# Score blocks sharing one tile in the mixers of a two-layer diffusion trunk, with a reordered output projection

## The chip, the cores and the metric

The kernel runs on 1 core of one Trainium2 chip, as one launch. The metric is the device time of that launch in microseconds, lower is better. Every matmul works in fp32 or in the split form described below.

## The reference

One inference step of a trunk with two layers over 640 tokens (512 latent tokens of the sample, 128 context tokens of the prompt), width 1024. Layer 0 mixes tokens with HGRN2 (8 heads, 128 wide), layer 1 with GLA (4 heads, keys 128 wide, values 256 wide). Each mixer is a gated linear recurrence, run forward and backward, and followed by a gated norm over each head and an output projection; then comes PEER, a product-key layer of single-neuron experts. Cut to what matters here:

```
S_t = diag(exp(g_t)) S_{t-1} + k_t v_t^T ;  o_t = S_t^T q_t      (both directions, summed)
y   = o * rsqrt(mean(o*o over the head) + EPS) * w * silu(gate)  (_gated_head_norm)
x   = x + g1 * (y @ w_out)                                       (output projection)
q   = h @ w_q; top 16 of keys per half and head; 16 of the 256 sums; gates = softmax
x   = x + g2 * sum_e gates_e * gelu(u_e . h) * v_e               (PEER)
```

Outputs are the two normed token blocks and the final states of the context scans.

## The kernel before, in words

Tokens stand in five tiles of 128 (`NT` = 5, the last is the context), the width in eight chunks of 128 (`DC` = 8). The stages run one after the other, each in a block of its own, with a barrier between: setup, then for each layer a mixer, `mix_out`, retrieve, route and experts, and finish at the end. A product that needs fp32 precision at a faster rate is split: both factors are cut into a high part and a low rest, both float32r, and three matmuls (high by high, high by low, low by high) add up in PSUM.

**Mixer.** A loop runs over the heads (`pe.Fori`, L1163), each engine in its own written order. For a head, TensorE projects this head and part of the next, transposes, updates the states, and then does the attention. Inside a tile of 128 tokens the decayed scores are not one product. For each of seven levels (64, 32, 16, 8, 4, 2, 1) there is a pair of factors in `ex`, exact for token pairs whose indices differ first in that bit; `scores(t)` (L1132) makes seven full 128x128 products (L1137) and one for the diagonal (L1138), side by side in `pA[t % 2]`. VectorE multiplies all eight tiles at once by 0/1 masks in `level_mask` (L1048), into `am`. TensorE then takes the eight masked tiles, for each of `NV` value chunks (1 in HGRN2, 2 in GLA), as eight accumulating matmuls against the turned values, and two more against the states (L1154). The order is scores(0), scores(1), outputs(0), scores(2), outputs(1) and so on. ScalarE copies each output tile away (L856). After its last mask VectorE goes on with the decays of the next head (L966, then scans).

**`mix_out`.** ScalarE and VectorE square alternate chunks of the mixer output into two buffers `sq`; TensorE sums them by one-column matmuls into `rows` (L1291), all 8 (or 4) heads; VectorE inverts, ScalarE roots. `spread(g)` (L1301) turns the root of head g into a full tile by 5 fp32 matmuls. VectorE multiplies by it and by the norm weight (L1350), then by the gate (L1364), ScalarE takes the high part (L1272), VectorE the low (L1358). The gate is made by ScalarE's sigmoid (L1255, two buffers `sg`) and GpSimd (L1233). The product with `w_out` (L1308) runs in two ways: for the first `AHEAD` = 3 of eight column groups TensorE follows the chunks k as they come (18 matmuls of 320 columns per k); the other five follow group by group (48 matmuls each), with weights split by ScalarE (L1248) and GpSimd (L1228) into three buffers.

**Experts.** At the start TensorE turns the context tokens of h row-wise: 32 transposes of `h_hi` and `h_lo` (L2069), whose halves VectorE copies and adds (L1982, L1984) in turn; then the first u block is transposed (L2127), and the main loop runs over 128 blocks of experts. At its end ScalarE (L1964) and VectorE (L2049) copy the six halves of `py`, TensorE transposes them (L2142), VectorE adds to x (L2054), ScalarE squares it (L1969) and GpSimd sums the squares in `acc` (L1926), with a drain behind each of its seven additions.

Of the kernel before, what the change touches and what calls it, by code (L numbers as in the profile page):

```python
# [15 lines left out]
P = 128  # L16
# [11 lines left out]
NL = len(LEVELS)  # L28
DEPTH = 2
# [5 lines left out]
TG = 2  # L35
# [63 lines left out]
def build_program(nc, a, out, upto=99):  # L99
# [6 lines left out]
    with ctx:  # L106
        c = {}
        for name, shape, dt in [
            ("ident", [P, P], F32), ("ones_d", [P, P], F32), ("ones_h", [P, P], F32),
            ("level_mask", [P, (NL + 1), P], BF16), ("scan_f", [P, T], BF16), ("scan_b", [P, T], BF16),  # L110
            ("vec", [P, 3 * P], F32), ("mod", [P, DEPTH, 48, 2], F32), ("one", [P, 1], F32),
            ("scale_w", [P, DC, 2], F32), ("lb", [P, 16], F32), ("oml", [P, 16], F32),
# [49 lines left out]
def setup(nc, a, c, x_sp, x_saved):  # L162
# [4 lines left out]
    with ExitStack() as s:  # L167
# [81 lines left out]
        def _(act):  # L249
# [3 lines left out]

            for g in range(3 + 10):
# [8 lines left out]
        def _(dve):  # L263
# [6 lines left out]
            for l, m in enumerate(LEVELS):  # L270
                nc.vector.tensor_scalar(low[:, :], xorf[:, :], float(m), None, ALU.is_ge)
                dve.drain()
                nc.vector.scalar_tensor_tensor(c["level_mask"][:, l, :], xorf[:, :], float(2 * m), low[:, :],
                                               ALU.is_lt, ALU.mult)
                dve.drain()
            nc.vector.tensor_scalar(c["level_mask"][:, NL, :], xorf[:, :], 0.0, None, ALU.is_equal)
# [220 lines left out]
def mixer(nc, a, c, mx, h_hi, h_lo, og_sp, out, layer, x_saved):  # L497
# [19 lines left out]
    with ExitStack() as s:  # L517
# [17 lines left out]
        am = [sb(f"am{i}", [P, NL + 1, P]) for i in range(2)]  # L535
# [352 lines left out]
        def _(dve):  # L888
# [81 lines left out]
            def head(h, final):  # L970
# [73 lines left out]
                for t in range(NT):  # L1044
# [3 lines left out]
                    nc.vector.tensor_mul(am[t % 2][:, :, :], pA[t % 2][:, :, :], c["level_mask"][:, :, :]) \  # L1048
# [21 lines left out]
        def _(pe):  # L1070
# [24 lines left out]
            def head(h, final):  # L1095
# [36 lines left out]
                def scores(t):  # L1132
# [3 lines left out]
                    for l in range(NL):  # L1136
                        nc.tensor.matmul(pA[t % 2][:, l, :], ex[:, 1, l, tok], ex[:, 0, l, tok], start=True, stop=True)  # L1137
                    nc.tensor.matmul(pA[t % 2][:, NL, :], kd[:, tok], q[:, tok], start=True, stop=True) \  # L1138
# [3 lines left out]
                for t in range(NT):  # L1142
# [5 lines left out]
                    for vv in range(NV):  # L1148
                        dst = pO[:, vv, :]
                        terms = [(tt[:, 10 + t * NV + vv, :], am[t % 2][:, l, :]) for l in range(NL + 1)]  # L1150
# [18 lines left out]
def mix_out(nc, a, c, mx, h_hi, h_lo, og_sp, x_sp, layer):  # L1169

    NV, H = mx.nv, mx.heads
    AHEAD = 3
    w_out = a["gla_w_out" if mx.gla else "hgrn_w_out"][0].rearrange("(k p) n -> p k n", p=P)
    gw = VEC["gla_g" if mx.gla else "hgrn_g"]
    oT, inv = c["x"], c["inv"][:, 0:H * NT]
    with ExitStack() as s:
# [5 lines left out]
        sg = [sb(f"sg{i}", [P, T]) for i in range(2)]  # L1182
        sq = [sb(f"sq{i}", [P, T]) for i in range(2)]
# [4 lines left out]
        spread_s = ps("spread_s", [P, 4, P])  # L1188
        spread_c = ps("spread_c", [P, P])
        pp = [[ps(f"pp{j}_{i}", [P, 512]) for i in range(2)] for j in range(AHEAD)]  # L1190
        (sq_act, sq_dve, summed, inverted, rooted, spread_done, spread_read, sig_done, gate_done, y_done, hi_done,
         lo_done, w_hi_done, w_lo_done, proj, added, x_ready, squared) = (sem(n) for n in (
            "sq_act", "sq_dve", "summed", "inverted", "rooted", "spread_done", "spread_read", "sig_done", "gate_done",
# [5 lines left out]
        rows = pp[0][0][:, 0:H * NT]  # L1199

        @block.sync
        def _(sp):
# [20 lines left out]
        def _(pool):  # L1223
# [11 lines left out]
            for k in range(DC):  # L1235
                gate(k)
                if k < AHEAD:
                    low(k)
# [998 lines left out]
```

## Time and profile before

| | |
|---|---|
| median of 3 runs | 4647.11 us (4644.31 to 4648.92) |
| the profiled execution, its own time | 4647.06 us |
| its span in the trace | 4645.2 us |
| mixer, layer 0 and layer 1 | 568.4 and 460.9 us |
| `mix_out`, layer 0 and layer 1 | 124.0 and 115.9 us |
| experts, layer 0 and layer 1 | 1221.7 and 1220.2 us |
| setup, retrieve, route and finish together | 934.1 us |

The stages stand in a row, so their times add up to the span. The engine columns of the page are busy time over the whole span; inside a stage the bound changes from place to place, and timelines of the stage show it. A timeline row gives the start in us, the duration, the engine, the line, the operation with output and inputs, the shapes and, in brackets, the idle time before it with the instruction that ended it. PE is TensorE, PEld its weight load, DVE VectorE, ACT ScalarE, POOL GpSimd.

### The profile page before, as it was taken

Reading aid. Unit: us, or ns where it says so; the run is one execution under the profiler, and the core shown is the slowest. Engines: PE = TensorE matmul, PEld = TensorE weight load, DVE = VectorE, ACT = ScalarE, POOL = GpSimd, SP = SyncE. Lnnn points to the kernel's source line nnn. Section 1 sums busy time; section 2 is a strip of 40 time slices with the busy share of each in tenths; the row PEclk is TensorE's granted clock in tenths of the full one; section 3 lists DMA queues with packets and bytes.
Section 4 is the critical chain, followed back from the end, with each engine's and each line's share of the span. In section 5 each row is a group of like instructions: output and inputs, shape, how many; then the busy total and the mean of one; then the engine's idle time right before and its main releaser. Section 6 shows DMA issues by size and latency. Waiting matters only on the chain. (4 is left out here: it accounts for less than half of the span.)

```text
span 4645.2 us, 72467 instructions
## 1 busy us (share of the span) xinstructions
PE 4146.5 (89%) x24511; PEld 3755.6 (81%) x24511; DVE 3803.5 (82%) x6733; ACT 1642.9 (35%) x2307; POOL 1991.1 (43%) x1435
## 2 busy tenths in 40 slices
PE   7799986877799999999996888786889999999997
PEld 3599986875699999999986778785779999999996
DVE  7688884599788888999996876378978888899997
ACT  7545442213233333333334432221323333333333
POOL 3234331215454545566544221220744545565663
PEclk9899998888899999999997988897999999999998
DMA  9411112214999999999972110220699999999995
GB/s 368 146 46 55 54 33 74 60 31 91 270 366 360 364 360 358 366 362 362 363 281 81 38 40 20 82 66 16 148 316 363 362 362 363 356 365 363 361 361 207
DMA packets 616027, 1049.49 MB, mean 226 GB/s; under 512 B 229699, under 2 KB 388870, under 8 KB 615430
## 3 DMA queue, kind: packets, MB, share of 16 engines
q1 hardware_dynamic: 467814, 508.86, 32.4%
q0 software_dynamic: 147456, 536.94, 31.1%
q10 hardware_dynamic: 672, 2.62, 0.2%
q8 instruction: 46, 0.75, 0.1%
q14 instruction: 39, 0.32, 0.0%
HBM read 982.75 MB, written 65.54 MB: 226 GB/s over the span
## 5 line engine op out<-in xcount | busy, mean ns | idle before, releaser
L1920 POOL DMA_INDIRECT rows_ex<-in_peer_v,ctx_index x512 | 707.6, 1382 | 475.5 <-DVE row_acc_ex L1999 359.9
L1920 POOL DMA_INDIRECT rows_ex<-in_peer_u,ctx_index x512 | 588.0, 1148 | 645.4 <-DVE dots_ex L2002 501.7
L2088 PE MATMUL pu_ex<-h_hi,uT_hi_ex 128*128 128x384 f32 x2048 | 715.6, 349 | 1.9 <-ACT coef_ex L1944 1.0
L1999 DVE SCALAR_TENSOR_TENSOR row_acc_ex<-rows_ex,factor_ex,row_acc_ex 128x1024 f32<-128x1024 f32 x512 | 657.6, 1284 | 52.8 <-issue 11.1
L2088 PE MATMUL pu_ex<-h_hi,uT_lo_ex 128*128 128x384 f32 x2048 | 692.6, 338 | 0.0
L2088 PE MATMUL pu_ex<-h_lo,uT_hi_ex 128*128 128x384 f32 x2048 | 692.5, 338 | 0.0
L2096 PE MATMUL py_ex<-v_hi_ex,c_hi_ex 128*128 128x512 f32 x1536 | 622.4, 405 | 0.0
L2002 DVE CUSTOM_DVE_ANT_0 rows_ex<-rows_ex,h_row_ex 128x1024 f32<-128x1024 f32 x512 | 604.3, 1217 | 0.0
L2096 PE MATMUL py_ex<-v_lo_ex,c_hi_ex 128*128 128x512 f32 x1536 | 601.0, 391 | 0.0
L2096 PE MATMUL py_ex<-v_hi_ex,c_lo_ex 128*128 128x512 f32 x1536 | 600.6, 391 | 0.0
L1933 ACT ACTIVATE uT_hi_ex<-pT_ex 128x512 fp32r<-128x512 f32 x512 | 304.1, 594 | 575.1 <-PE pT_ex L2081 473.0
L1990 DVE TENSOR_TENSOR uT_lo_ex<-pT_ex,uT_hi_ex 128x512 fp32r<-128x512 f32 x512 | 351.7, 687 | 166.4 <-ACT uT_hi_ex L1933 153.7
L1939 ACT ACTIVATE v_hi_ex<-v_raw_ex 128x1024 fp32r<-128x1024 f32 x256 | 271.7, 1061 | 485.8 <-PE py_ex L2096 485.8
L2088 PEld LDWEIGHTS pu_ex<-h_hi,uT_hi_ex 128*128 128x128 f32 x2048 | 385.9, 188 | 12.8 <-DVE uT_lo_ex L1990 1.5
L2088 PEld LDWEIGHTS pu_ex<-h_lo,uT_hi_ex 128*128 128x128 f32 x2048 | 386.3, 189 | 9.8
L2088 PEld LDWEIGHTS pu_ex<-h_hi,uT_lo_ex 128*128 128x128 f32 x2048 | 385.4, 188 | 0.0
L2096 PEld LDWEIGHTS py_ex<-v_lo_ex,c_hi_ex 128*128 128x128 f32 x1536 | 288.3, 188 | 63.8
L2096 PEld LDWEIGHTS py_ex<-v_hi_ex,c_lo_ex 128*128 128x128 f32 x1536 | 289.5, 188 | 42.9
L2096 PEld LDWEIGHTS py_ex<-v_hi_ex,c_hi_ex 128*128 128x128 f32 x1536 | 288.8, 188 | 42.4
L2013 DVE TENSOR_TENSOR v_lo_ex<-v_raw_ex,v_hi_ex 128x1024 fp32r<-128x1024 f32 x256 | 311.7, 1218 | 0.0
L2081 PE MATMUL pT_ex<-ident,u_raw_ex 128*128 128x128 f32 x2040 | 306.1, 272 | 3.1 <-issue 3.1
L2081 PEld LDWEIGHTS pT_ex<-ident,u_raw_ex 128*128 128x128 f32 x2040 | 253.7, 140 | 46.5 <-issue 3.7
(418 smaller groups left out, 8599.6 us busy)
## 6 DMA issues: line engine op xcount, KB each, us to landing
u_raw_ex<-in_peer_u SPq DMA_DIRECT2D x256, 512.0 KB
v_raw_ex<-in_peer_v SPq DMA_DIRECT2D x256, 512.0 KB
ada<-in_ada_w SPq DMA_DIRECT2D x24, 2048.0 KB, 10.0
gates<-stage_ro SPq DMA_DIRECT2D x12, 4096.0 KB, 23.3
g_raw_ex<-gates SPq DMA_DIRECT2D x256, 192.0 KB
w_raw_hgrn<-in_hgrn_w_in SPq DMA_DIRECT2D x40, 512.0 KB
w_raw_re<-in_peer_w_q SPq DMA_DIRECT2D x32, 512.0 KB, 3.7
w_raw_gla<-in_gla_w_in SPq DMA_DIRECT2D x25, 512.0 KB
```

Source lines behind the costliest of these rows:

```text
L1920: pool.indirect_dma_start(out=rows[m % RING][:, :], out_offset=None, in_=a["peer_u" if m < TG * NC else "peer_v"].rearrange("l n d -> (l n ...
L1933: act.activation(uT_hi[b][:, 4 * part:4 * part + 4, :], pT[:, :, :], ACT.Copy) \
L1939: act.activation(v_hi[b][:, :], v_raw[b][:, :], ACT.Copy).then_inc(v_hi_done, 1)
L1990: nc.vector.tensor_sub(uT_lo[b][:, at, :], pT[:, :, :], uT_hi[b][:, at, :].bitcast(F32)) \
L1999: nc.vector.scalar_tensor_tensor(row_acc[g][:, :], rows[j][:, :], factor[:, j:j + 1], row_acc[g][:, :], ALU.mult, ALU.add).then_inc(row_fr ...
L2002: nc.vector.tensor_tensor_reduce(rows[j][:, :], rows[j][:, :], h_row[g][:, :], 1.0, 0.0, ALU.mult, ALU.add, accum_out=dots[:, j:j + 1]).th ...
L2013: nc.vector.tensor_sub(v_lo[b][:, :], v_raw[b][:, :], v_hi[b][:, :].bitcast(F32)).then_inc(v_lo_done, 1)
L2081: last_ = nc.tensor.transpose(pT[:, k, :], u_raw[b][:, (4 * part + k) * P:(4 * part + k + 1) * P], c["ident"][:, :])
L2088: last_ = nc.tensor.matmul(pu[:, 0:TD], w[:, k, :], x[:, k, 0:TD], start=(k == 0 and w is uT_hi[b] and x is h_hi), stop=(k == DC - 1 and w ...
L2096: last_ = nc.tensor.matmul(py[2 * t + i][:, :], w[:, t * P:(t + 1) * P], x[:, i * HALF_D:(i + 1) * HALF_D], start=(first and w is c_hi[b] ...
```

## The change

Four places are edited.

1. **Mixer.** `scores(t)` puts levels 64, 32 and 16 into one tile, as eight smaller matmuls that write only the blocks which these levels own: two 64x64 blocks off the diagonal for level 64, two 64x64 blocks on it for level 32, and four 32x32 blocks on the diagonal over them for level 16. `level_mask`, `am` and the output terms have six tiles instead of eight.
2. **`mix_out`.** `AHEAD` is 2; each `sq` and `sg` has a buffer per chunk, so squares and sigmoids wait for no reader; the sums are made and rooted in two halves; `spread` has two buffers and runs two heads ahead; gate and norm weight are applied ahead on DVE (`gated`).
3. **Experts, start.** The 32 transposes become 32 float32r matmuls against `ident_r`, with high and low part added in PSUM, in four banks of their own; ScalarE copies them.
4. **Experts, end.** The copies of `y` are split three and three, the transposes begin after three of them and have four targets, GpSimd's additions carry their semaphore themselves, without the drain.

In route, the two `stage` buffers are allocated first, which moves addresses only.

```diff
-            ("level_mask", [P, (NL + 1), P], BF16), ("scan_f", [P, T], BF16), ("scan_b", [P, T], BF16),
+            ("level_mask", [P, NM, P], BF16), ("scan_f", [P, T], BF16), ("scan_b", [P, T], BF16),
...
+            nc.vector.tensor_scalar(c["level_mask"][:, 0, :], xorf[:, :], 16.0, None, ALU.is_ge)
...
-                    for l in range(NL):
-                        nc.tensor.matmul(pA[t % 2][:, l, :], ex[:, 1, l, tok], ex[:, 0, l, tok], start=True, stop=True)
+                    blocks = [(0, 64 * b, 64 - 64 * b, 64) for b in range(2)] + [(1, 64 * b, 64 * b, 64) for b in range(2)]
+                    blocks += [(2, 32 * b, 32 * b, 32) for b in range(4)]
+                    for l, r, col, n in blocks:
+                        nc.tensor.matmul(pA[t % 2][r:r + n, 0, col:col + n], ex[:, 1, l, t * P + r:t * P + r + n],
+                                         ex[:, 0, l, t * P + col:t * P + col + n], start=True, stop=True)
+                    for l in range(3, NL):
+                        nc.tensor.matmul(pA[t % 2][:, l - 2, :], ex[:, 1, l, tok], ex[:, 0, l, tok], start=True, stop=True)
...
-    AHEAD = 3
+    AHEAD = 2
+    GROUP = H // 2
...
             gates(0)
+            gates(1)
             weights(0)
             weights(1)
-            gates(1)
-            weights(2)
             gates(2)
...
+            for g in range(GROUP):
+                sums(g)
             spread(0)
+            spread(1)
+            for g in range(GROUP, H):
+                sums(g)
             for k in range(DC):
-                if k % NV == NV - 1 and k // NV + 1 < H:
-                    spread(k // NV + 1)
-                if k == 0:
-                    pe.wait_ge(w_lo_done, AHEAD)
                 pe.wait_ge(lo_done, k + 1)
                 for j in range(AHEAD):
+                    if k == 0:
+                        pe.wait_ge(rooted, j + 1)
+                        pe.wait_ge(w_lo_done, j + 1)
...
+                if k % NV == NV - 1 and k // NV + 2 < H:
+                    spread(k // NV + 2)
...
+            def gated(k):
+                dve.wait_ge(gate_done, k + 1)
+                nc.vector.scalar_tensor_tensor(oT[:, k, :], oT[:, k, :], c["vec"][:, gw + k % NV:gw + k % NV + 1],
+                                               og[:, k, :], ALU.mult, ALU.mult)
...
             for k in range(DC):
                 normal(k)
-                dve.wait_ge(gate_done, k + 1)
-                dve.drain()
-                nc.vector.tensor_mul(y[k % 3][:, :], y[k % 3][:, :], og[:, k, :]).then_inc(y_done, 1)
+                if k == 0:
+                    inverse(1)
+                if k + 3 < DC:
+                    gated(k + 3)
                 if k >= 1:
                     low(k - 1)
+                dve.drain()
...
-                pool.tensor_tensor(c["acc"][:, :], c["acc"][:, :], rows[k % 2][:, 0:T], ALU.add)
-                pool.drain().then_inc(gathered, 1)
+                if k >= 2:
+                    pool.wait_ge(gathered, k - 1)
+                pool.tensor_tensor(c["acc"][:, :], c["acc"][:, :], rows[k % 2][:, 0:T], ALU.add).then_inc(gathered, 1)
...
-                for w, part in enumerate((h_hi, h_lo)):
-                    for k in range(4):
-                        last_ = nc.tensor.transpose(py[2 * (n % 2) + w][:, k * P:(k + 1) * P],
-                                                    part[:, 4 * half + k, tok].bitcast(F32), c["ident"][:, :])
+                for k in range(4):
+                    for w, part in enumerate((h_hi, h_lo)):
+                        last_ = nc.tensor.matmul(py[n][:, k * P:(k + 1) * P], part[:, 4 * half + k, tok],
+                                                 c["ident_r"][:, :], start=(w == 0), stop=(w == 1))
```

The order of ScalarE in `mix_out` is now: the squares, sigmoids 0 to 3, the high parts of weight groups 0 and 1, sigmoids 4 to 7, the first root, the high part of chunk 0, the second root, then the other high parts.

TensorE, first attention of HGRN2, before and of the change (`pA` holds the scores, `pO` the outputs):

```order
L1137 MATMUL pA_hgrn<-ex_hgrn 128x128 x7
L1138 MATMUL pA_hgrn<-q_hgrn,kdiag_hgrn 128x128
L1137 MATMUL pA_hgrn<-ex_hgrn 128x128 x7
L1138 MATMUL pA_hgrn<-q_hgrn,kdiag_hgrn 128x128
L1145 REGISTER_ALU
L1154 MATMUL pO_hgrn<-am_hgrn,tt_hgrn 128x128 x8
L1154 MATMUL pO_hgrn<-e_hgrn,S_hgrn 128x128 x2
```

```order
L1145 MATMUL pA_hgrn<-ex_hgrn 64x64 x4
L1145 MATMUL pA_hgrn<-ex_hgrn 32x32 x4
L1148 MATMUL pA_hgrn<-ex_hgrn 128x128 x4
L1149 MATMUL pA_hgrn<-q_hgrn,kdiag_hgrn 128x128
L1145 MATMUL pA_hgrn<-ex_hgrn 64x64 x4
L1145 MATMUL pA_hgrn<-ex_hgrn 32x32 x4
L1148 MATMUL pA_hgrn<-ex_hgrn 128x128 x4
L1149 MATMUL pA_hgrn<-q_hgrn,kdiag_hgrn 128x128
L1156 REGISTER_ALU
L1165 MATMUL pO_hgrn<-am_hgrn,tt_hgrn 128x128 x6
L1165 MATMUL pO_hgrn<-e_hgrn,S_hgrn 128x128 x2
```

Three full products of a score call have become eight small ones, and two output terms are gone.

TensorE in the first `mix_out`, from the sums to the first products, before and of the change:

```order
L1291 MATMUL pp_0_mo<-ones_d,sq_mo 128x1 x40
L1301 MATMUL spread_s_mo<-ident,inv 128x128 x4
L1301 MATMUL spread_c_mo<-ident,inv 128x128
L1301 MATMUL spread_s_mo<-ident,inv 128x128 x4
L1301 MATMUL spread_c_mo<-ident,inv 128x128
L1308 MATMUL pp_0_mo<-h_hi,w_hi_mo 128x320
L1308 MATMUL pp_0_mo<-h_lo,w_hi_mo 128x320
```

```order
L1297 MATMUL pp_0_mo<-ones_d,sq_mo 128x1 x20
L1306 MATMUL spread_s_mo<-ident,inv 128x128 x4
L1306 MATMUL spread_c_mo<-ident,inv 128x128
L1306 MATMUL spread_s_mo<-ident,inv 128x128 x4
L1306 MATMUL spread_c_mo<-ident,inv 128x128
L1297 MATMUL pp_0_mo<-ones_d,sq_mo 128x1 x20
L1313 MATMUL pp_0_mo<-h_hi,w_hi_mo 128x320
L1313 MATMUL pp_0_mo<-h_lo,w_hi_mo 128x320
```

The second half of the sums now stands behind the first two spreads.

## Rows read from the trace of the kernel before

**Rows 1.** The page: busy time, share of the span and instructions of each engine

```profile
PE 4146.5 (89%) x24511; PEld 3755.6 (81%) x24511; DVE 3803.5 (82%) x6733; ACT 1642.9 (35%) x2307; POOL 1991.1 (43%) x1435
```

**Rows 2.** Timeline of PE, hgrn attention of one head (start us, us, instruction, idle before)

```profile
392.41 1.80 PE L1137 MATMUL pA_hgrn<-ex_hgrn 128*128 128x128 f32 x14 [0.86 <-DVEq L1043]
...
394.27 1.73 PE L1137 MATMUL pA_hgrn<-ex_hgrn 128*128 128x128 f32 x14
...
396.05 1.95 PE L1154 MATMUL pO_hgrn<-am_hgrn,tt_hgrn 128*128 128x128 f32 x16
```

**Rows 3.** Timeline of DVE there: the mask multiply

```profile
408.31 1.23 DVE L1048 TENSOR_TENSOR am_hgrn<-pA_hgrn,level_mask 128x1024 f32<-128x1024 f32 x1 [2.01 <-PE pA_hgrn L1138]
```

**Rows 4.** Timeline of PE, gla attention: two score calls in turn

```profile
2592.65 1.73 PE L1137 MATMUL pA_gla<-ex_gla 128*128 128x128 f32 x14
...
2598.90 1.73 PE L1137 MATMUL pA_gla<-ex_gla 128*128 128x128 f32 x14
```

**Rows 5.** Timeline of PE in setup, where small and full tiles alternate

```profile
142.15 1.05 PE L378 MATMUL pc<-fold,mod_row 4*128 4x2 f32 x8
143.13 1.09 PE L389 MATMUL pa<-ada_hi,cs 128*4 128x512 f32 x4
```

**Rows 6.** Groups of weight loads in setup, by form (busy us, mean ns)

```profile
L378 PEld LDWEIGHTS pc<-fold,mod_row 4*128 4x128 f32 x8 | 1.0, 186 | 0.5 <-issue 0.5
L389 PEld LDWEIGHTS pa<-ada_lo,cs 128*4 128x4 f32 x8 | 0.6, 84 | 1.4 <-DVE ada_lo L313 0.6
```

**Rows 7.** Engines' busy time in mix_out's first stretch; last PEclk, DMA share, GB/s

```profile
730.60:749.70 19.10, 17.19 (x90) 16.81 (x90) 3.91 (x7) 7.04 (x9) 0.48 (x1) 0.59 0.96 357
```

**Rows 8.** Timeline of PE in mix_out

```profile
731.39 14.68 PE L1291 MATMUL pp_mo<-ones_d,sq_mo 128*128 128x1 f32 x80 [2.03 <-ACT sq_mo L1260]
...
762.48 0.63 PE L1308 MATMUL pp_mo<-h_hi,w_hi_mo 128*128 128x320 f32 x1 [9.22 <-POOL w_lo_mo L1228]
...
767.44 1.49 PE L1301 MATMUL spread_s_mo<-ident,inv 128*128 128x128 f32 x8
...
780.14 0.42 PE L1308 MATMUL pp_mo<-h_hi,w_hi_mo 128*128 128x320 f32 x1 [2.75 <-DVE h_lo L1358]
...
782.88 1.05 PE L1301 MATMUL spread_s_mo<-ident,inv 128*128 128x128 f32 x8
...
786.91 0.42 PE L1308 MATMUL pp_mo<-h_hi,w_hi_mo 128*128 128x320 f32 x1 [2.75 <-DVE h_lo L1358]
...
814.66 0.41 PE L1308 MATMUL pp_mo<-h_hi,w_hi_mo 128*128 128x320 f32 x1 [1.91 <-POOL w_lo_mo L1228]
```

**Rows 9.** Timeline of DVE in mix_out, one step of the k loop

```profile
790.97 0.75 DVE L1350 SCALAR_TENSOR_TENSOR y_mo<-x,vec,spread_s_mo 128x512 f32<-128x512 f32 x1 [4.11 <-PE spread_c_mo L1301]
791.63 0.34 DVE L1350 SCALAR_TENSOR_TENSOR y_mo<-x,vec,spread_c_mo 128x128 f32<-128x128 f32 x1
792.06 0.82 DVE L1364 TENSOR_TENSOR y_mo<-y_mo,og_mo 128x640 f32<-128x640 f32 x1
792.81 0.82 DVE L1358 TENSOR_TENSOR h_lo<-y_mo,h_hi 128x640 fp32r<-128x640 f32 x1
```

**Rows 10.** Timeline of PE in mix_out, second layer

```profile
2952.06 0.64 PE L1308 MATMUL pp_mo<-h_hi,w_hi_mo 128*128 128x320 f32 x1 [12.82 <-POOL w_lo_mo L1228]
```

**Rows 11.** Timeline of PE at the start of experts

```profile
1230.56 1.09 PE L2069 MATMUL py_ex<-ident,h_hi 128*128 128x128 f32 x4 [9.66 <-PEq L57]
...
1239.02 0.81 PE L2127 MATMUL pT_ex<-ident,u_raw_ex 128*128 128x128 f32 x4 [2.04 <-issue]
```

**Rows 12.** Timeline of ACT after the last product of experts

```profile
2426.27 2.06 ACT L1964 ACTIVATE u_raw_ex<-py_ex 128x512 f32<-128x512 f32 x4 [6.45 <-PE py_ex L2096]
```

**Rows 13.** Timeline of POOL at the end of experts

```profile
2432.22 1.54 POOL L1926 TENSOR_TENSOR acc<-acc,rows_ex 128x640 f32<-128x640 f32 x1 [22.16 <-ACT rows_ex L1969]
2441.16 1.54 POOL L1926 TENSOR_TENSOR acc<-acc,rows_ex 128x640 f32<-128x640 f32 x1 [7.40 <-issue]
2442.87 1.53 POOL L1926 TENSOR_TENSOR acc<-acc,rows_ex 128x640 f32<-128x640 f32 x1 [0.18 <-issue]
```

More of the change, by code:

```diff
@@ L28 @@
 NL = len(LEVELS)
+NM = NL - 1
 DEPTH = 2
@@ L534, in mixer @@
         ex = sb("ex", [P, 2, NL, T])
-        am = [sb(f"am{i}", [P, NL + 1, P]) for i in range(2)]
+        am = [sb(f"am{i}", [P, NM, P]) for i in range(2)]
         tt = sb("tt", [P, NTR, P])
@@ L1149, in head @@
                         dst = pO[:, vv, :]
-                        terms = [(tt[:, 10 + t * NV + vv, :], am[t % 2][:, l, :]) for l in range(NL + 1)]
+                        terms = [(tt[:, 10 + t * NV + vv, :], am[t % 2][:, l, :]) for l in range(NM)]
                         if t < NT - 1:
@@ L1181, in mix_out @@
         og = sb("og", [P, DC, T])
-        sg = [sb(f"sg{i}", [P, T]) for i in range(2)]
-        sq = [sb(f"sq{i}", [P, T]) for i in range(2)]
+        sg = sb("sg", [P, DC, T])
+        sq = sb("sq", [P, DC, T])
         y = [sb(f"y{i}", [P, T]) for i in range(3)]
@@ L1198, in mix_out @@
         block = s.enter_context(nc.Block())
-        rows = pp[0][0][:, 0:H * NT]
+        rows = [pp[j][0][:, 0:GROUP * NT] for j in range(2)]
+        inv = [c["inv"][:, j * GROUP * NT:(j + 1) * GROUP * NT] for j in range(2)]
         @block.sync
@@ L1229, in low @@
                                    w_hi[j % AHEAD][:, :, :].bitcast(F32), ALU.subtract).then_inc(w_lo_done, 1)
-            def gate(k):
+            for k in range(DC):
                 pool.wait_ge(sig_done, k + 1)
-                pool.tensor_tensor(og[:, k, :], og[:, k, :], sg[k % 2][:, :], ALU.mult).then_inc(gate_done, 1)
[L1235 to L1238, printed above, removed]
+                pool.tensor_tensor(og[:, k, :], og[:, k, :], sg[:, k, :], ALU.mult).then_inc(gate_done, 1)
+                if k in (1, 2):
+                    low(k - 1)
             for j in range(AHEAD, DC):
@@ L1285, in _, with sums @@
         def _(pe):
-            for g in range(H):
+            def sums(g):
                 for k in range(g * NV, (g + 1) * NV):
@@ L1579, in route @@
         ALLC = [P, NT, PH, TOPK]
+        stage = [sb(f"stage{i}", [P, KEYS, STORE]) for i in range(2)]
         e = sb("e", ALLC)
@@ L1598, in route @@
             [shared[:, i * UNIT * P:(i + 1) * UNIT * P].rearrange("p (u n) -> p u n", n=P) for i in range(2)]
-        stage = [sb(f"stage{i}", [P, KEYS, STORE]) for i in range(2)]
         pg = [ps(f"pg{i}", [P, UNIT, P]) for i in range(2)]
```

155 lines of the change are left out of this document (78 added, 77 removed).

## The prediction

> **What bounds the kernel now.** I read the page first, then stage by stage the timelines of the engines. TensorE is busy 89% of the span [rows 1], but that is a mean over stages: in the expert loops it never stops and the change leaves them alone. The edits touch four places, and what counts there is who is waited for.
>
> In the HGRN2 attention TensorE runs without a gap from score call to score call: a call starts at 394.27 and its outputs at 396.05, so a call takes 1.79 us for 16 fp32 passes (a full fp32 matmul is two passes in the trace), 0.112 us each; before the phase it has idled 0.86 us for VectorE [rows 2]. The phase leads somewhere: the last mask, 1.23 us on VectorE [rows 3], releases the decays of the next head, a chain that ends in those 0.86 us. So this head's time from first score to last mask is on the path, TensorE's work behind it is not. In GLA one token tile takes 6.25 us (2592.65 to 2598.90, [rows 4]), all TensorE, and the next projection waits for the end of the phase, so there all of it is on the path.
>
> `mix_out` is bound by latencies. It begins with DMA at 0.96 of its share and a granted clock of 0.59, a mix of 2.4 GHz and 1.2 GHz [rows 7]. TensorE makes its sums from 731.39 for 14.68 us, has spread the first head by 749.70 (the stretch of [rows 7] ends there), later waits 9.22 us for the low weights from GpSimd and starts its first product at 762.48. In the k loop it is idle 2.75 us of a step of 6.77 us (780.14 to 786.91) for `h_lo`, since spread, norm, gate, high and low follow each other [rows 8].
>
> **The change, part by part.** The sum is made against the profiled execution, 4647.06 us by its own time, span 4645.2; the median shown is 4647.11, so the two can be taken as one. 0.2%, about what a measurement of this kernel can tell from no change, is 9.3 us.
>
> *Score calls.* Removed: three full matmuls, 6 passes, 0.67 us. Added: eight matmuls on 64 columns and on 32, 16 passes. The trace shows no such matmul. If a pass shrinks with its columns, 8 x 0.056 + 8 x 0.028 = 0.67 us: nothing won or lost. To this comes the change of tile shape: in setup, eight passes of another shape take 0.98 us from start (142.15) to the next row (143.13) where 8 x 0.112 would be 0.89, so about 0.09 us for a change of shape [rows 5]. A call has three such changes (full to 64, 64 to 32, 32 to full): 0.27 us. The weight load is no reason for more: it takes 84 ns for 4 columns and 186 ns for 128 [rows 6], so it shrinks with the columns too. I take +0.4 us per call, c below: 0.27, and something for calls that run at 1.2 GHz and for passes that shrink less than their columns. Bounds: if blocks for different output partitions run side by side, 8 + 8 passes cost as 4 + 2 or so, about 0.30, and c is 0.30 + 0.27 - 0.67 = -0.1; if no pass falls below a full one, c is 10 x 0.112 + 0.27 = +1.39.
>
> The Trainium skill ("TensorEngine Tiling (Array Packing)", Key Properties) says that changing the tiling mode drains TensorE; this trace agrees, with about 0.09 us a change. The Trainium skill ("TensorE: Matmul & The Clock Gate", Part 3: Packing small matmuls) says that matmuls on different column tiles overlap; that is rival B, and where the sum has -7 us for the mixers, -37 would stand. No row here shows two blocks at once.
>
> *Mask and outputs.* The mask works on 768 instead of 1024 columns: 1.23 us becomes about 0.93, 0.30 less. Outputs lose two matmuls per value chunk, 4 passes, 0.45 us. In HGRN2 between first score and last mask lie five score calls, three output groups and the last mask: 5c - 3 x 0.45 - 0.30 = 5c - 1.64 per head, 8 heads. In GLA, TensorE alone counts: 5c - 5 x 2 x 0.45 = 5c - 4.48, 4 heads. Together 60c - 31 us; **with c = 0.4, -7 us**. The masks in setup cost nothing: VectorE waits there for inputs.
>
> *`mix_out`, first layer.* The start gets no shorter. ScalarE now does all eight sigmoids and two weight copies before its root, but that ends no later than the sums and the loads let it: I put the first root at 747.4: the sums end at 746.07 now (731.39 + 14.68), and the root follows a microsecond later. At 1.2 GHz two spreads follow, 2.6 us each, and 40 passes of sums at 0.213, 8.5 us: 761.1. Then inverse, root, norm and low of VectorE (one step costs 0.75 + 0.34 + 0.82 + 0.82 us [rows 9]) give the first product at 765.4, 3 us later than before. Step 0 of the loop takes 3.2 + 2.6 us, step 1 3.2 + 1.4 (12 matmuls, and a spread), the next four 1.76 + 1.37 each (12 x 0.147, which is what 6.77 - 2.75 - 1.37 leaves for each of 18, and a spread of 1.37 us with its start-up [rows 8]), the last two 1.76: 26.4 us. Gone are the idle 2.75 us per step, since two heads are spread ahead and gates are applied ahead; late next is VectorE at 2.7 us a step, which stays under 3.1. Loop end 791.8. Then a wait for weights, 1.91 us before at 814.66 [rows 8], with two buffers about 2.9, then six groups instead of five, 48 x 0.147 = 7.04 us each, 42.3; three us for the last sums of x: 840, where the stage ended at 854.6. **-14.6 us**. The trade is a group of column work moved from the loop (it filled idle time there) to the end, +7, against a loop of 26 instead of 50 us.
>
> *`mix_out`, second layer.* Here a head has two chunks. The first product stands at 2952.06 [rows 10], 37.8 us into the stage, and comes at the same 34.8 us as above, 2949.1. The loop is then bound by VectorE, eight steps of 2.7 and the ends: 23 us. With 2.9 + 42.3 + 3 the stage ends at 3019.8 instead of 3030.1, **-10.3 us**.
>
> *Start of experts.* TensorE needs from 1230.56 for groups of four transposes about 0.86 us each, with stops for VectorE's adds, and starts on u at 1239.02 after 2.04 us of idle time [rows 11]. A float32r matmul is one quick pass: in `mix_out` 18 of them with 320 columns fill 762.48 to 767.44 at 1.2 GHz [rows 8], 0.27 us each, so 128 columns take about 0.11, where a transpose takes 0.21 ((1.09 - 0.45) / 3 in the group of four). With the loads I take 0.13 us for each of 32, and nothing waits between: done at about 1234.9, and u has landed. **-4.1 us per layer, -8.2**; the copies on ScalarE lie beside the transposes of u. The expert loop behind is TensorE's alone, so the shift comes through.
>
> *End of experts.* ScalarE copies four halves in 2.06 us [rows 12]; TensorE now starts after two, 1.0 us earlier. GpSimd's first addition starts at 2432.22 and the second at 2441.16, 7.40 us after it has ended, though ScalarE's squares come every 1.1 us; the later ones are 1.71 apart, with 0.18 between [rows 13]. What stands between the first two is the drain. Without drains the adds follow at about 1.6, but the block ends with one, and I suppose that GpSimd pays there what it paid at the first: something that the gathers left to be cleared. Then 1.0 + 6 x 0.11 is all: **-1.7 us per layer, -3.4**. If it vanishes, 7.2 us more per layer.
>
> **Sum:** -7 - 14.6 - 10.3 - 8.2 - 3.4 = -43.5, from 4647.06: **4603.5 us**.
>
> **The rivals.**
>
> *The drain's price goes away* (A). For it: the wait sits right behind the first drain and nowhere else, as if the drain itself were at fault. Against: it would be long even if only the gathers' remains were waited for, and somebody must wait for them. It gives 2 x 7.2 less, 4589.
>
> *Blocks run side by side* (B). For it: they write different partitions; against: no row shows it, and the two 64-column blocks of level 64 and those of level 32 alternate over the same partitions. c = -0.1, mixers -37 instead of -7: 4573.
>
> *The loop of `mix_out` gains nothing* (C). For it: TensorE's second sums stand before the first product, ScalarE's sigmoids before the first root; if the gates' loads come late, both slip, and GpSimd's gates slow VectorE in the loop. Against: DMA is done by 749 and GpSimd's gates now begin 10 us earlier. Without the 25: 4628.
>
> *Slower: small passes cost full ones* (D). Each of the 16 passes takes 0.112 us plus three changes of shape, c = 1.39 and 60c - 31 = +52: 4663. It decides from c = 1.28 on, where the mixers' loss passes the 36.5 us won elsewhere by 9.3. For it: in setup eight passes of two columns take 0.98 us, no less than full ones would. Against: those have weights of 128 columns and 0.112 is then the load; here the weights have 64 or 32, and loads of 4 columns take less than half.
>
> *It does not do what it says* can hardly be: the written orders show the blocks and the six terms. A scheduler stands nowhere between.
>
> **How the numbers follow.** My sum 0.55, A 0.18, B 0.09, C 0.10, D 0.06, no effect 0.02. The range takes in A, B and C, and the unknown c up to about 0.9: 4570 to 4632. Faster by over 0.2% needs c under 0.97 with the rest as summed, or c under 0.55 without `mix_out`: 0.89; within 0.2% 0.05; slower 0.06.
>
> **What would show it.** Right: a score call of about 2.2 us in HGRN2, blocks' rows of some 0.03 to 0.06 us apart, the period 4.0 (+0.4 - 0.45); first product of `mix_out` 35 us into the stage and steps of 3.1 us; in experts u transposed from 1235 less what came before; on GpSimd seven additions without a hole, and a long drain at the end of the block. Wrong: score calls over 3 us, or under 1.8; a first product of `mix_out` later than 40 us; retrieve, route or the expert loop of another length than before.

## The result, and the profile after

The changed kernel takes 4583.27 us (median of 4 runs, 4577.81 to 4585.24) against 4647.7 us; the ratio is 0.9861, 95% interval [0.9844, 0.9878]. That is 64 us less, where 43.5 were forecast. The profiled execution took 4584.52 us by its own time, span 4582.7.

```profile
span 4582.7 us, 73015 instructions
PE 4118.9 (90%) x24791; PEld 3713.0 (81%) x24791; DVE 3765.7 (82%) x6718; ACT 1645.2 (36%) x2314; POOL 1991.2 (43%) x1435
```

These are the page's lines that answer to [rows 1]. They say little: 280 more PE records, 28 us less busy. The stages say it all. Each is taken from its first to its last record in both traces:

| stage | before | after | difference | forecast |
|---|---|---|---|---|
| mixer, layer 0 | 568.4 | 560.4 | -8.0 | +2.9 |
| `mix_out`, layer 0 | 124.0 | 120.9 | -3.1 | -14.6 |
| route, layer 0 | 171.3 | 161.8 | -9.5 | 0 |
| experts, layer 0 | 1221.7 | 1220.7 | -1.0 | -5.8 |
| mixer, layer 1 | 460.9 | 446.7 | -14.2 | -9.9 |
| `mix_out`, layer 1 | 115.9 | 103.7 | -12.2 | -10.3 |
| route, layer 1 | 172.0 | 161.6 | -10.4 | 0 |
| experts, layer 1 | 1220.2 | 1218.9 | -1.3 | -5.8 |
| setup, retrieve, finish, and the steps between stages | 590.8 | 588.0 | -2.8 | 0 |

(The forecast of the mixers is its formula at c = 0.4: 8 x 0.36 and 4 x -2.48.) The total came out near because an edit that I had costed at nothing, the place of route's buffers, gave 20 us, while `mix_out` in layer 0 and the experts gave little of what they were to give. A stage in a single trace is good to some 3 us: in six traces whose mixers are the same code (the change and experiments 1, 2, 6, 7 and 8) the first takes 557.3 to 560.4 us and the second 443.7 to 447.0.

**The score call.** TensorE in one HGRN2 attention, the answer to [rows 2]:

```profile
392.23 0.65 PE L1145 MATMUL pA_hgrn<-ex_hgrn 128*64 128x64 f32 x16
392.81 1.16 PE L1148 MATMUL pA_hgrn<-ex_hgrn 128*128 128x128 f32 x8
393.81 0.39 PE L1149 MATMUL pA_hgrn<-q_hgrn,kdiag_hgrn 128*128 128x128 f32 x2
394.03 1.50 PE L1165 MATMUL pO_hgrn<-am_hgrn,tt_hgrn 128*128 128x128 f32 x12
395.37 0.61 PE L1165 MATMUL pO_hgrn<-e_hgrn,S_hgrn 128*128 128x128 f32 x4
395.91 0.28 PE L1145 MATMUL pA_hgrn<-ex_hgrn 128*64 128x64 f32 x2
```

From the first of the 16 block passes to the first full pass behind them it is 0.58 us (392.23 to 392.81), 0.036 us each: less than the 0.67 us that passes one after another would need, even with no price for a change of shape. The single records of this call show why. The 64-column passes start in pairs 0.007 us apart (four pairs, 0.05 to 0.10 us between), the 32-column passes in two groups of four, each 0.007 us apart. So blocks on different output partitions run side by side. Changes of shape are dearer than I had: the first block starts 0.205 us behind the last full pass and not 0.112, the first 32-column pass 0.15 us behind the last 64-column one, the first full pass 0.126 us behind the last block, and the second full pass 0.214 us behind the first: some 0.39 us in all. Both together: a period from score call to score call of 3.68 us (392.23 to 395.91) where before it was 4.02; without the two output terms (0.45) it would have been 3.57, so c is +0.11.

**Route.** This is the view of the DMA queues over route in layer 0, first of the kernel before, then of the changed one (the stretch in 40 slices, busy tenths of the queues and GB/s):

```profile
DMA  0000000000002999999999999999999999999997
GB/s 4 0 2 0 0 0 0 0 0 4 0 0 56 218 217 218 218 216 218 217 218 216 219 219 218 218 216 217 218 218 215 218 217 218 218 215 218 220 217 172
DMA packets 98405, 25.22 MB, mean 147 GB/s; under 512 B 98400, under 2 KB 98400, under 8 KB 98400
...
gates<-stage_ro SPq DMA_DIRECT2D x6, 4096.0 KB, 23.3
```

```profile
DMA  0000000000000599919997699919997799919996
GB/s 0 0 0 2 0 4 0 0 0 0 0 0 0 134 290 290 290 33 286 290 290 170 150 290 291 290 25 290 290 290 160 165 290 290 289 30 290 290 288 147
DMA packets 98405, 25.22 MB, mean 156 GB/s; under 512 B 98400, under 2 KB 98400, under 8 KB 98400
...
gates<-stage_ro SPq DMA_DIRECT2D x6, 4096.0 KB, 16.0
```

The same 98400 pieces of 256 bytes go out at 290 GB/s where it was 218; a transfer of 4 MB takes 16.0 us and not 23.3. Before, the queues were full from the first store to the stage's end, and ScalarE waited for the buffer. Now the DMA has pauses, and the stage is set by VectorE, busy 147.3 us of its 161.8.

**The loop of `mix_out`.** TensorE and VectorE in two steps of layer 0, the answers to [rows 8, 9]:

```profile
779.13 0.42 PE L1313 MATMUL pp_mo<-h_hi,w_hi_mo 128*128 128x320 f32 x1 [1.71 <-DVE h_lo L1368]
...
781.00 1.05 PE L1306 MATMUL spread_s_mo<-ident,inv 128*128 128x128 f32 x8
781.89 0.39 PE L1306 MATMUL spread_c_mo<-ident,inv 128*128 128x128 f32 x2
783.99 0.41 PE L1313 MATMUL pp_mo<-h_hi,w_hi_mo 128*128 128x320 f32 x1 [1.71 <-DVE h_lo L1368]
```

```profile
782.31 0.69 DVE L1363 TENSOR_TENSOR y_mo<-x,spread_s_mo 128x512 f32<-128x512 f32 x1 [3.24 <-PE spread_c_mo L1306]
782.91 0.28 DVE L1363 TENSOR_TENSOR y_mo<-x,spread_c_mo 128x128 f32<-128x128 f32 x1
783.11 0.82 DVE L1368 TENSOR_TENSOR h_lo<-y_mo,h_hi 128x640 fp32r<-128x640 f32 x1
```

The first product came at 752.88, 31.4 us into the stage (34.8 forecast), but the loop to the last product took until 792.62: 39.7 us instead of 26.4. A step takes 4.86 us (779.13 to 783.99), and 5.65 to 7.21 us in the four steps before, while gates are still applied. The rows show a chain that leads through both engines: VectorE's low part, for which TensorE waits at 783.99, ends at 783.93; it stands behind the norm at 782.31, which waits for the spread that ends at 782.28, and TensorE makes that spread only behind the products of the step before.

**Both ends of the experts.** TensorE at the start and GpSimd at the end, layer 0 [rows 11, 13]:

```profile
1214.93 0.41 PE L2089 MATMUL py_ex<-ident_r,h_hi 128*128 128x128 f32 x1
1215.14 0.41 PE L2089 MATMUL py_ex<-ident_r,h_lo 128*128 128x128 f32 x1
1215.36 1.07 PE L2146 MATMUL pT_ex<-ident,u_raw_ex 128*128 128x128 f32 x4
```

```profile
2409.44 1.54 POOL L1954 TENSOR_TENSOR acc<-acc,rows_ex 128x640 f32<-128x640 f32 x1 [21.24 <-ACT rows_ex L1998]
2411.13 9.93 POOL L1954 TENSOR_TENSOR acc<-acc,rows_ex 128x640 f32<-128x640 f32 x6 [0.15 <-POOL acc L1954]
2429.63 0.31 POOL L699 MEMSET wg_gla<- 128x256 f32 x1 [8.57 <-POOLq L58]
```

A float32r matmul of 128 columns starts every 0.213 us at 1.2 GHz, exactly as a transpose did, so the 32 take 6.9 us (1208.49 to 1215.36). On GpSimd the hole between the first two additions is gone, and it has come back as 8.57 us behind the last.

### The profile page after: what moved, and what is told of

Same layout as the page of the kernel before. It is cut to its first block and busy times, and to the rows that moved or that the text cites. A ratio compares the mean times of both kernels' runs of the same rounds, so it can differ in the third digit from the quotient of the medians.

```text
span 4582.7 us, 73015 instructions
## 1 busy us (share of the span) xinstructions
PE 4118.9 (90%) x24791; PEld 3713.0 (81%) x24791; DVE 3765.7 (82%) x6718; ACT 1645.2 (36%) x2314; POOL 1991.2 (43%) x1435
## 5 line engine op out<-in xcount | busy, mean ns | idle before, releaser
L2021 DVE SCALAR_TENSOR_TENSOR row_acc_ex<-rows_ex,factor_ex,row_acc_ex 128x1024 f32<-128x1024 f32 x512 | 657.6, 1284 | 52.7 <-issue 11.1
```

The costliest lines, as they stand in the source:

```text
L2021: nc.vector.scalar_tensor_tensor(row_acc[g][:, :], rows[j][:, :], factor[:, j:j + 1], row_acc[g][:, :], ALU.mult, ALU.add).then_inc(row_fr ...
```

## The experiments

Ratios are to the kernel before, run on the same chip. Differences in us between an experiment and the change are taken from the ratios (one hundredth is 46.5 us), since the experiments ran on different chips. The interval of each ratio reaches about 8 us to either side, so a difference of two ratios is good to about 11 us (an estimate from these intervals); what is finer than that is read from the stages.

**1. Where the stage buffers lie.** The change with a pad of 32 bytes, and the kernel before with a pad of 96.

```diff
+        sb("pad", [P, 8])
         stage = [sb(f"stage{i}", [P, KEYS, STORE]) for i in range(2)]
```

> The change with one edit: 32 bytes per partition are allocated ahead of route's two stage buffers, so that they begin 32 bytes past a multiple of 256 and not on one (before the change they began 160 past). Theory (the alignment of the 256-byte pieces that the transfer reads sets its rate): 290 GB/s fall back to about 218, route takes 171 us again instead of 161.7, in both layers: about 4603, +20. Rival (it is the place in memory, low or high, and not the alignment): route stays at 161.7 and the time at 4583.

Measured 4603.24 us (4595.47 to 4614.45), ratio 0.991 [0.9892, 0.9928]: +23 us against the change. Route takes 172.1 us in both layers, and the rate is back:

```profile
GB/s 0 0 2 0 0 4 0 0 0 0 0 0 30 217 218 217 218 216 218 218 218 216 218 219 218 218 215 218 217 218 215 218 218 217 218 215 220 221 217 174
```

```diff
+        sb("pad", [P, 24])
         stage = [sb(f"stage{i}", [P, KEYS, STORE]) for i in range(2)]
```

> The kernel before with one edit: 96 bytes per partition are allocated ahead of route's stage buffers, which stay last, so that they begin on a multiple of 256 bytes and not 160 past it. Theory (alignment): transfers at 290 GB/s, route 161.7 instead of 171.3 and 172.0 us, about 4628, -20. Rival (the low place in memory, or the order of allocation): no change.

Measured 4625.12 us (4623.2 to 4628.45), ratio 0.9956 [0.994, 0.9973]: -20 us against before, with route at 160.9 and 161.1 us and 290 GB/s again:

```profile
GB/s 4 0 2 0 0 0 0 0 0 0 4 0 0 127 290 290 290 46 272 290 290 191 128 290 291 290 46 267 290 290 195 128 290 290 290 44 274 290 292 189
```

The two runs settle from both sides that it is the alignment of the address, and neither the place in memory nor the order of allocation. A remainder of 32 by 256 costs as much as one of 160. Both of these are also 32 past a multiple of 128 and of 64, so the runs don't show whether a multiple of 64 or 128 bytes would do as well as one of 256.

**2. The order on VectorE in `mix_out`.**

```diff
             for k in range(DC):
+                if k >= 1:
+                    low(k - 1)
                 normal(k)
                 if k == 0:
                     inverse(1)
                 if k + 3 < DC:
                     gated(k + 3)
-                if k >= 1:
-                    low(k - 1)
                 dve.drain()
```

> The change with VectorE's loop in mix_out reordered: low(k - 1) stands ahead of normal(k) and no longer behind it. Theory (the loop's steps of 4.9 to 7.2 us come from low(k - 1) queued behind normal(k), which waits for a spread that TensorE makes only after the products of step k - 2): steps fall to about 3.2 us, layer 0's loop from 39.7 to 27 us, some 2 us in layer 1: about 4569, -14. Rival (ScalarE's high part and VectorE's own work set the step): steps stay above 4.5 us and the time within 4 us of 4583.

Measured 4557.8 us (4553.67 to 4562.7), ratio 0.9805 [0.9788, 0.9821]: -26 us, more than expected. The loop's step:

```profile
757.89 1.05 PE L1306 MATMUL spread_s_mo<-ident,inv 128*128 128x128 f32 x8
758.78 0.39 PE L1306 MATMUL spread_c_mo<-ident,inv 128*128 128x128 f32 x2
758.93 0.41 PE L1313 MATMUL pp_mo<-h_hi,w_hi_mo 128*128 128x320 f32 x1
...
760.79 0.38 PE L1306 MATMUL spread_s_mo<-ident,inv 128*128 128x128 f32 x2
```

From spread to spread it is 2.90 us, no idle time between, and TensorE is the bound in this step. `mix_out` takes 102.3 and 99.5 us, 18.6 and 4.2 less than in the change. In layer 0 the loop went from 39.7 to 24.8 us (747.66 to 772.49): that is the reordering. The first product came 2.1 us earlier (29.3 us into the stage), and the six groups behind the loop took 42.5 us at a granted clock of 1.00 where the change took 44.0 at 0.96. The groups' gain isn't the reordering's: experiment 1, with the slow loop of 39.7 us, has 42.5 us at 1.00 too. 3 us of the profiled difference lie in the first mixer (557.3 against 560.4), whose code is the same; that is scatter.

**3. The scores of before.**

```diff
-NM = NL - 1
+NM = NL + 1
...
-                    for l in range(3, NL):
-                        nc.tensor.matmul(pA[t % 2][:, l - 2, :], ex[:, 1, l, tok], ex[:, 0, l, tok], start=True, stop=True)
+                    for l in range(NL):
+                        nc.tensor.matmul(pA[t % 2][:, l, :], ex[:, 1, l, tok], ex[:, 0, l, tok], start=True, stop=True)
```

> The change with the scores of before: seven full levels and the diagonal, eight masks, eight output terms; all else of the change stays. Theory (the difference of the mixer stages, -8.0 and -14.2 us, is the score tile's work alone): the mixers return to 568 and 461 us, about 4605, +22. Rival (part of it is drift or addresses): +15 or less.

Measured 4607.19 us (4596.18 to 4608.0), ratio 0.9903 [0.9886, 0.9919]: +20 us. The mixers are back at 568.8 and 461.5 us, 23.2 more than in the change; the ratios alone would not exclude the rival's 15.

**4. All blocks 32 columns wide.**

```diff
-                    blocks = [(0, 64 * b, 64 - 64 * b, 64) for b in range(2)] + [(1, 64 * b, 64 * b, 64) for b in range(2)]
+                    blocks = [(0, 32 * b, 64 - 64 * (b // 2), 64) for b in range(4)]
+                    blocks += [(1, 32 * b, 32 * (b + 1 - 2 * (b % 2)), 32) for b in range(4)]
...
-                        nc.tensor.matmul(pA[t % 2][r:r + n, 0, col:col + n], ex[:, 1, l, t * P + r:t * P + r + n],
+                        nc.tensor.matmul(pA[t % 2][r:r + 32, 0, col:col + n], ex[:, 1, l, t * P + r:t * P + r + 32],
```

> The change with all three block levels made of matmuls with 32 weight columns (level 64 as four with 64 moving columns, levels 32 and 16 as four each with 32), so that a score call changes the tile shape twice and not three times. Theory (a change of shape costs about 0.1 us and blocks on different output partitions run side by side, four at a time): each call loses 0.10 us for the change and some 0.05 us of passes, 60 calls: about 4575, -8. Rival (passes run one after another): 24 passes of 32 or 64 columns cost 0.2 us more per call than now: +12.

Measured 4566.23 us (4556.19 to 4572.02), ratio 0.982 [0.9802, 0.9838]: -19 us. The mixers take 551.0 and 442.4 us.

```profile
391.12 0.44 PE L1146 MATMUL pA_hgrn<-ex_hgrn 128*32 128x64 f32 x24
391.50 1.16 PE L1149 MATMUL pA_hgrn<-ex_hgrn 128*128 128x128 f32 x8
...
394.60 0.32 PE L1146 MATMUL pA_hgrn<-ex_hgrn 128*32 128x64 f32 x8
```

From the first of the 24 passes to the full pass behind them it is 0.38 us, where the change needed 0.58 for 16; the period is 3.48 us and not 3.68. One after another, eight passes of 64 columns and sixteen of 32 would be 8 x 0.056 + 16 x 0.028 = 0.90 us. 60 calls by 0.20 us are 12 us, and the two mixers together are shorter by 13.7. What is above (5 us) lies in stages whose code is the same and within what two ratios can tell.

**5. A change of shape more.**

```diff
+                    put(blocks[:4])
                     for l in range(3, NL):
                         nc.tensor.matmul(pA[t % 2][:, l - 2, :], ex[:, 1, l, tok], ex[:, 0, l, tok], start=True, stop=True)
+                        if l == 4:
+                            put(blocks[4:])
```

> The change with the same matmuls in another order inside a score call: the four 64x64 blocks, two full levels, the four 32x32 blocks, two full levels, the diagonal. That makes four changes of tile shape where the change has three. Theory (each change costs about 0.1 us, plus about 0.1 us on the first full pass behind small ones): 60 calls by 0.1 to 0.2 us, +6 to +12, 4589 to 4595. Rival (the 0.1 us are the start of a series and no change of shape): the same 4583.

Measured 4599.79 us (4595.86 to 4607.84), ratio 0.9901 [0.9886, 0.9916]: +19 us, above the range expected but not clear of it, by the 11 us above. The rival, no change, is out.

```profile
390.53 0.45 PE L1146 MATMUL pA_hgrn<-ex_hgrn 128*64 128x64 f32 x8
390.91 0.71 PE L1150 MATMUL pA_hgrn<-ex_hgrn 128*128 128x128 f32 x4
391.55 0.27 PE L1146 MATMUL pA_hgrn<-ex_hgrn 128*32 128x32 f32 x8
391.75 0.71 PE L1150 MATMUL pA_hgrn<-ex_hgrn 128*128 128x128 f32 x4
392.30 0.39 PE L1153 MATMUL pA_hgrn<-q_hgrn,kdiag_hgrn 128*128 128x128 f32 x2
```

The same passes now take 1.77 us from the first block to the diagonal (390.53 to 392.30), 1.58 in the change (392.23 to 393.81): +0.19 us a call, 11.6 us for 60. Four full passes fill 0.64 us (390.91 to 391.55) and not 0.45: 0.1 us goes at the second pass, 0.1 at the next change. The mixers are longer by 5.6 and 4.3 us in the profiled run, 10 together; 2 us more are in `mix_out`, whose code is the same, so some of the 19 us is not the order's.

**6. GpSimd's drain, earlier.**

```diff
                     .then_inc(row_in[m % RING], 16)
+            pool.drain()
             for k in range(1, DC):
```

> The change with a drain of GpSimd right after its last gather in experts, some 20 us before its first addition. Theory (what a drain waits for after the gathers is paid once, by the first drain that comes, and lasts about 8 us from that drain on): the drain at the end of the block gets short, 7 us less per layer: about 4569, -14. Rival (every drain behind additions costs it, or the price is the gathers' remains at the end of the block whatever was drained ahead): no change.

Measured 4563.36 us (4562.27 to 4568.19), ratio 0.9826 [0.9809, 0.9842]: -16 us. Experts take 1211.2 and 1211.1 us, 9.5 and 7.8 less; from their last product to the end of the stage it is 7.2 us less in both layers. The same rows as above, of this kernel:

```profile
2405.80 9.93 POOL L1955 TENSOR_TENSOR acc<-acc,rows_ex 128x640 f32<-128x640 f32 x6 [0.15 <-POOL acc L1955]
2417.01 0.31 POOL L699 MEMSET wg_gla<- 128x256 f32 x1 [1.28 <-POOLq L58]
```

The 8.57 us are down to 1.28, and the additions have no hole either. The drains' own records say the same. In the change the closing drain ends at 2428.34, 7.3 us behind the last addition, though the last gather had landed at 2392.89. Here the early drain ends at 2391.18, 8.3 us behind the last gather's instruction, and the closing one follows its addition within 0.1 us. The price is paid once, at the first drain behind the gathers, and here it lies in the 21 us in which GpSimd waits for its first square. What the drain does in that time is not shown.

**7. The `mix_out` of before**, whole, in the changed kernel.

```diff
-    AHEAD = 2
+    AHEAD = 3
...
```

> The change with the mix_out of before, all else as in the change. Theory (the stages' differences of -3.1 and -12.2 us are mix_out's own): about 4598, +15. Rival (some of it comes from what stands around it, as the clock that the mixer leaves): under +8 or over +22.

Measured 4597.85 us (4595.43 to 4600.44), ratio 0.9896 [0.988, 0.9913]: +16 us. But by stage it is 121.0 and 119.5 us: the new `mix_out` gives nothing in layer 0 in this pair of traces and 15.8 us in layer 1. One pair says little here. The old one takes 121.0 to 125.5 and 115.9 to 119.5 us in three traces (before, experiment 7 and the pad of 96 in experiment 1), the new one 118.1 to 126.0 and 99.0 to 103.9 in seven (the change and experiments 1, 3, 4, 5, 6 and 8): by the means some 2 us less in layer 0, within the scatter, and 14 in layer 1.

**8. A wider identity.** 24 of the 32 matmuls at the start of experts get 256 moving columns, of which the second half is zero.

```diff
-                        last_ = nc.tensor.matmul(py[n][:, k * P:(k + 1) * P], part[:, 4 * half + k, tok],
-                                                 c["ident_r"][:, :], start=(w == 0), stop=(w == 1))
+                        cols = slice(k * P, min(k + 2, 4) * P)
+                        last_ = nc.tensor.matmul(py[n][:, cols], part[:, 4 * half + k, tok],
+                                                 c["ident_r"][:, 0:min(2, 4 - k) * P], start=(w == 0), stop=(w == 1))
```

> The change with an identity of 256 columns (the second half zero) in the 32 float32r matmuls at the start of experts: 24 of them have 256 moving columns and 8 have 128, where all had 128; the later matmuls overwrite the zeros. In the change such a matmul of 128 columns starts every 0.213 us at 1.2 GHz, one of 320 in mix_out every 0.267. Theory (a float32r matmul of 128 columns takes two cycles a column and one of 256 or more takes one): the pitch stays 0.213 us with 256 columns. Rival (the pitch is set by the weight load or by cycles per column as such): the same 0.213 by the load, or 0.43 by two cycles a column. The time stays at 4583 or rises by at most 12.

One run, 4579.68 us.

```profile
1211.73 0.41 PE L2091 MATMUL py_ex<-ident_r,h_hi 128*128 128x256 f32 x1
1211.94 0.41 PE L2091 MATMUL py_ex<-ident_r,h_lo 128*128 128x256 f32 x1
...
1212.37 0.41 PE L2091 MATMUL py_ex<-ident_r,h_lo 128*128 128x256 f32 x1
1212.58 0.31 PE L2091 MATMUL py_ex<-ident_r,h_hi 128*128 128x128 f32 x1
1212.69 0.41 PE L2091 MATMUL py_ex<-ident_r,h_lo 128*128 128x128 f32 x1
1212.90 0.52 PE L2091 MATMUL py_ex<-ident_r,h_hi 128*128 128x256 f32 x1
1213.22 0.41 PE L2091 MATMUL py_ex<-ident_r,h_lo 128*128 128x256 f32 x1
```

256 columns start every 0.213 us, as 128 did, at a granted clock of 0.50 (1.2 GHz). The number that I expected came, but it can't tell my theory (two cycles a column for narrow float32r) from the load of the weights. The two matmuls of 128 columns in these rows can. The second starts 0.107 us behind the first (1212.58 and 1212.69), one cycle a column at 1.2 GHz and not two. The time is not won: from 1212.37 to 1213.22 four matmuls take 0.85 us, 0.213 each, so the moving columns are not what sets the pace. Another row, of the changed kernel, shows what does: the sums of `mix_out`, layer 1, second half, which move one column past 128 columns of fp32 weights, at the same granted clock:

```profile
2898.29 8.53 PE L1297 MATMUL pp_mo<-ones_d,sq_mo 128*128 128x1 f32 x40
```

40 of them in 8.53 us are 0.213 us each as well. One, 128 or 256 moving columns make no difference in the mean; what the three have in common is the load of 128 weight columns of 4 bytes, and that is the floor. At 320 columns the moving columns count (0.27 us [rows 8]). My theory falls, the rival stands. The Trainium skill ("TensorE: Matmul & The Clock Gate", LDWEIGHTS (loading the stationary operand)) says that a load's time goes with the number of weight columns and not with the contraction rows. This case agrees: 128 columns on 4 partitions load in 186 ns [rows 6], 128 on 128 partitions in 192 ns in the score calls of the change, and 64 and 32 columns there in 136 and 108 ns.

One thing here was not expected. The start of the experts, to the first product of the loop, is 8.7 and 8.6 us and not 10.6: the granted clock is at 1.00 (2.4 GHz) from about 1215.5 on, where the change has 0.50 for as long as this start lasts, and the last matmuls of 256 columns start 0.118 us apart. One run can't show that the whole time gains by it.

**9. The three edits together** (2, 4 and 6).

> The change with three edits together: VectorE's low ahead of normal in mix_out, all three block levels with 32 weight columns, GpSimd's drain after its last gather. Alone they gave 25, 17 and 20 us against 4583. Theory (they sit in different stages and add up): about 4521. Rival (part of each gain was drift between calls): 4535 or more.

Measured 4532.48 us (4520.9 to 4538.27, 5 runs), ratio 0.9752 [0.9739, 0.9765]: 115 us below before, 51 below the change. It beats both kernels. By ratios the single gains are 26, 19 and 16, together 61. The rival (4535 or more) is not excluded: 51 and 61 are apart by less than the ratios can tell, and the spread of these five runs, 17 us, is wide. In its profiled execution, the fastest of the five, the mixers take 549.8 and 434.4 us, `mix_out` 103.1 and 99.0, the experts 1211.5 and 1211.0.

## Why the prediction was right, and where not

The direction was right, and the time lay within its range; that it came so near the sum was partly luck. In the traces the change is 62.4 us shorter, 18.9 more than forecast. Route gave 19.9 us that were not forecast, the mixers 15.2 more than forecast, and `mix_out` in layer 0 and the experts together 20.8 less. The prediction's own signs of being wrong say so too: route was to keep its length, and a score call, forecast at 2.2 us, takes 1.80 (392.23 to 394.03), the edge of "under 1.8".

- **Score calls** (forecast c = +0.4). The path was right, the terms of c were not. The passes do not shrink with their columns one by one: they run side by side, which was rival B, 9 in 100, and the sixteen take 0.39 us (0.11 - 0.39 + 0.67) where the sum had 0.67. And changes of shape cost 0.39 us a call and not 0.27, since I took the price from two rows of setup [rows 5] that miss the slow second pass behind a change. The one nearly pays for the other, c = +0.11. With 60c - 31 that is -24 us; measured -22.2 by the stages, -20 by experiment 3 (good to 11 us), whose mixers are back at their old times. The formula (which passes lie on the path in which layer) held, also in its split: 8 x (0.55 - 1.64) = -9 and 4 x (0.55 - 4.48) = -16 against -8.0 and -14.2. Rival D, slower, was far off: its argument from passes of two columns in setup had weights of 128 columns, as the text said against it.
- **`mix_out`, layer 0** (forecast -14.6, came -3.1). The step that failed: "Gone are the idle 2.75 us per step, since two heads are spread ahead". The spread was ahead on TensorE, but `low(k - 1)` was queued behind `normal(k)` on VectorE, in its written order, and so waited for a spread that TensorE makes only behind the products of k - 2. Those products, `spread(k)`, `normal(k)`, `low(k - 1)` and the products of k - 1 followed one another, and TensorE idled 1.71 us of a step of 4.86. The diff showed that order. Experiment 2 puts the step at 2.90 us (3.1 forecast) once it is turned round, and the loop at 24.8 us (26.4 forecast). A part of rival C, then, by another mechanism than the one it named: neither gates nor loads were late.
- **`mix_out`, layer 1** (forecast -10.3, came -12.2). Right: with two chunks a head, only every second step waits for a spread, and the loop takes 20.3 us (23 forecast). By its own terms the sum ended at 3020.3 and not 3019.8, which is -9.8.
- **Route** (forecast 0, came -19.9). The step that failed: the move of the buffers was taken for addresses only, and I wrote in no place what a transfer of 256-byte pieces does at another address. In the changed kernel the buffers begin at a multiple of 256 bytes, before they began 160 past one. The Trainium skill ("DMA: Bandwidth & Descriptors", How a descriptor splits into AXI transactions) says that when a descriptor does not start 256-byte-aligned, its first transaction starts at the 256-byte boundary below, so that bytes before the start are fetched too. For a piece of 256 bytes that makes two transactions of one (worked out from the page). This case agrees in direction, with 218 against 290 GB/s, and it is the rule that would have spoken for this edit. It does not agree with the page's count of beats, by which (an estimate) 160 bytes past the boundary would cost 13 and 32 bytes past 9 against 8, where the rate is 218 GB/s in both.
- **Start of experts** (forecast -4.1 per layer). The mechanism was right (no waits between, TensorE goes on to u at once), the size was off: 0.213 us a matmul instead of 0.13. From stage start to the first product of the loop it was 11.8 us and is 10.6, in layer 1 11.1 and 10.6: -1.2 and -0.6. I scaled the 0.27 us of 320-column matmuls down to 128 moving columns and put 0.02 us on top for the loads, where the load of 128 weight columns is a floor of 0.213 us (experiment 8). The sums in [rows 8], one column each, 80 in 14.68 us (0.18 each, at a mix of both clocks), pointed to that floor.
- **End of experts** (forecast -1.7 per layer, came -1.2 in both, last product to the end of the stage). Right, and with its reason: the drain's price moved to the end of the block. Experiment 6 shows that it belongs to the first drain behind the gathers. Rival A fell.
- The expert loop between took 1.5 us more in layer 0 and 0.5 in layer 1 (1184.2 to 1185.7 and 1183.7 to 1184.2). That is within its scatter: in eight other traces with the changed experts (all but experiment 8) it takes 1183.4 to 1185.9 and 1183.5 to 1184.8. What makes the same code scatter so, and the first mixer by 3 us, stays open.

## What to carry to other kernels

An operation that is prepared ahead on one engine is only ahead if every engine's written order lets it be: follow the chain of waits through all queues, and ask of each wait what useful work is queued behind it. Before a transfer of small pieces is costed at nothing because only its address moves, look at the address by 256 bytes. And the first drain behind GpSimd's gathers cost 7 to 8 us in every place it stood here, so put one where the engine is idle anyway.

## What was not expected of the hardware

- Full fp32 passes next to small ones: 0.09 us to start the first small pass, 0.09 us to start the first full one behind, and 0.10 us more for the second full pass, at 2.4 GHz.
- Passes with 32 weight columns on four different output groups start 0.007 us apart; from the first of 24 of them, with 64 or 32 moving columns, to the full pass behind it is 0.38 us.
- 256-byte reads from on-chip memory at an address 32 or 160 bytes past a multiple of 256 run at 218 GB/s, at a multiple at 290 (remainders between, as 64 and 128, were not tried).
- With 128 weight columns of fp32 or float32r a pass starts every 0.213 us in the mean at 1.2 GHz, whether 1, 128 or 256 columns move.
- A GpSimd drain behind indirect gathers that landed 26 us before still takes some 7 us (2421.06 to 2428.34 in the change), once.
